# Moving the shift of a normalised piece from GpSimd to ScalarE, and giving GpSimd more pieces

## What is computed

```python
def first_block(x, ...):
    h = rmsnorm(x, norm_mix_g)             # MIX
    x = x + mixer(h) @ w_out
    h = rmsnorm(x, norm_ffn_g)             # FFN
    x = x + (silu(dwconv(h @ w_gate)) * (h @ w_up)) @ w_down
    return rmsnorm(x, norm_final_g)        # FIN1

def second_block(x, c, ...):
    # a layer that pools, then a layer of attention; shift and scale come from c
    h = rmsnorm(x, norm_g[0]) * (1 + scale) + shift      # POOL (together with FIN1)
    x = x + gate * pool_mixer(h, ...)
    hk = rmsnorm(x, kv_norm_g) * (1 + scale) + shift     # KV
    k, v = split(hk @ w_kv)
    h = rmsnorm(x, norm_g[1]) * (1 + scale) + shift      # ATT
    x = x + gate * swa_sink_mixer(h, k, v, ...)
    return rmsnorm(x, final_g)                           # FIN2
```

## Time and profile before

| | |
|---|---|
| median of 3 runs | 2089.77 us (2089.43 to 2089.9) |
| the profiled execution | 2088.51 us |
| its span in the trace | 2086.8 us |
| PE busy | 2064.3 us, 99% |
| DVE busy | 1231.7 us, 59% |
| ACT busy | 650.7 us, 31% |
| POOL busy | 748.9 us, 36% |

### The profile page before, as it was taken

The page is one execution under the profiler, slowest core; times in us unless marked ns, Lnnn a source line. Parts: engine busy times, 40 slices in busy tenths (PEclk is TensorE's granted clock), DMA queues, the critical chain, the costliest instruction groups (busy, mean ns, idle before and its releaser), DMA issues.

```text
span 2086.8 us, 24768 instructions
## 1 busy us (share of the span) xinstructions
PE 2064.3 (99%) x9344; PEld 1694.1 (81%) x9344; DVE 1231.7 (59%) x1698; ACT 650.7 (31%) x1089; POOL 748.9 (36%) x441
## 2 busy tenths in 40 slices
PE   8999999999999999999999999999999999999998
PEld 7888888888888888888878888888888878777886
DVE  7999776555644456445676453453463570697565
ACT  7323345221122211222254122122121261676112
POOL 4555626222221222212276122122131462565623
PEclk9999999999999999999999999999999999999999
DMA  4231112322133222332112121121121120010202
GB/s 154 72 111 41 41 51 91 121 101 97 63 111 111 101 85 76 109 112 101 41 41 61 38 64 41 41 60 40 40 61 41 41 71 31 21 42 21 71 11 81
DMA packets 44749, 141.26 MB, mean 68 GB/s; under 512 B 5616, under 2 KB 9856, under 8 KB 44672
## 3 DMA queue, kind: packets, MB, share of 16 engines
q1 hardware_dynamic: 31632, 100.68, 15.1%
q10 hardware_dynamic: 13040, 39.54, 5.2%
HBM read 135.98 MB, written 7.36 MB: 69 GB/s over the span
## 4 chain that ended last, share of the span: by engine, by line
PE 80%; DVE 12%; POOL 4%; ACT 2%; issue 1%; DMA 0%; POOLq 0%; SPq 0%; ACTq 0%; DVEq 0%
PE psum L594 24%; PE psum L596 24%; PE psum L595 24%; DVE psum L1651 7%; POOL temp L444 2%; PE psum L932 1%; PE psum L943 1%; DVE psum L1504 1%; DVE norm_lo L1517 1%; POOL w_lo L409 1%; PE psum L911 1%; PE psum L661 1%; POOL ada_raw L444 0%; PE psum L663 0%; PE psum L662 0%
## 5 line engine op out<-in xcount | busy, mean ns | idle before, releaser
L409 POOL TENSOR_TENSOR w_lo<-w_raw,w_hi 128x1024 fp32r<-128x1024 f32 x174 | 441.6, 2554 | 972.5 <-ACT w_hi L1036 967.0
L594 PE MATMUL psum<-norm_hi,w_hi 128*128 128x512 f32 x1632 | 636.3, 390 | 0.3 <-ACT temp L1104 0.3
L596 PE MATMUL psum<-norm_hi,w_lo 128*128 128x512 f32 x1632 | 635.0, 389 | 0.0
L595 PE MATMUL psum<-norm_lo,w_hi 128*128 128x512 f32 x1632 | 634.9, 389 | 0.0
L594 PEld LDWEIGHTS psum<-norm_hi,w_hi 128*128 128x128 f32 x1632 | 306.4, 188 | 64.7 <-issue 0.9
L596 PEld LDWEIGHTS psum<-norm_hi,w_lo 128*128 128x128 f32 x1632 | 306.4, 188 | 63.8
L595 PEld LDWEIGHTS psum<-norm_lo,w_hi 128*128 128x128 f32 x1632 | 306.4, 188 | 63.3 <-issue 0.2
L1104 ACT ACTIVATE temp<-psum 128x512 f32<-128x512 f32 x160 | 93.9, 598 | 420.6 <-PE psum L596 393.7
L1567 DVE SCALAR_TENSOR_TENSOR stream<-psum,mods,stream 128x512 f32<-128x512 f32 x160 | 119.7, 750 | 172.5 <-PE psum L596 172.5
L1036 ACT CAST w_hi<-w_raw 128x1024 fp32r<-128x1024 f32 x158 | 159.2, 1047 | 138.8 <-PE psum L596 79.6
L1565 DVE TENSOR_TENSOR stream<-psum,stream 128x512 f32<-128x512 f32 x176 | 118.7, 689 | 83.8 <-PE psum L596 83.6
(11 more groups left out here) (214 smaller groups left out, 2974.7 us busy)
## 6 DMA issues: line engine op xcount, KB each, us to landing
w_raw<-in_slabs SPq DMA_DIRECT2D x175, 512.0 KB, 3.5
ada_raw<-in_ada ACTq DMA_DIRECT2D x10, 3072.0 KB, 12.6
stream<-in_x SPq DMA_DIRECT2D x8, 512.0 KB, 9.3
out<-stream SPq DMA_DIRECT2D x8, 512.0 KB, 2.8
skew_scratch<-row_scratch ACTq DMA_DIRECT2D x1, 3072.0 KB, 17.6
ada_raw<-in_ada ACTq DMA_DIRECT2D x1, 2048.0 KB, 7.9
bias<-skew_scratch ACTq DMA_DIRECT2D x4, 512.0 KB, 4.2
c_act<-in_c ACTq DMA_DIRECT2D x1, 512.0 KB, 9.7
```

The lines of the kernel that those rows point to most:

```text
L409: nc.gpsimd.tensor_tensor(WL[place][:, :], RAW[at % 2][:, :], WH[place][:, :].bitcast(f32), ALU.subtract).then_inc(slab_ready, 1)
L594: nc.tensor.matmul(dst, wh, xh, start=n == 0, stop=False)
L595: nc.tensor.matmul(dst, wh, xl, start=False, stop=False)
L596: last = nc.tensor.matmul(dst, wl, xh, start=False, stop=n == len(terms) - 1)
```

## The change

Five edits:

- The shift of a piece of `POOL_LOWS` is no longer added by POOL. ACT does it, in place, in an instruction of its own right behind the cast of the same piece; that instruction waits for this cast. POOL is left with one instruction for each such piece.
- `POOL_LOWS` grows: for FFN from 3 pieces to 5, for the pooling norm from 3 to 5, for KV from 3 to 5, for ATT from 4 to 7. They are now the odd pieces, from 7 on (in ATT from 1 to 13). POOL's program is laid out anew for them, and the low part of a weight slab stands behind the new pieces in places.
- In FIN2 the squares of pieces 14 and 15 go to two buffers that were free, so ACT no longer waits for POOL's sums there.
- POOL sums pieces 8 to 11 only. DVE adds the squares of 13 and 14 to that of 12, between its last additions to the stream. PE sums three tensors as before: POOL's sum, DVE's, and the square of 15.
- The second half of the result goes out in 8 transfers of one piece instead of 4 of two, piece 14 ahead of piece 13.

```diff
@@ squares, POOL_LOWS @@
+            if n == FIN2 and m > 13:
+                return body(T[1], m % 2)
...
-        POOL_LOWS = [(MIX, m) for m in (2, 4, 6, 9, 11, 13)] + [(FFN, m) for m in (9, 11, 13)] + [(POOL, m) for m in (9, 12, 15)]
-        POOL_LOWS += [(KV, m) for m in (9, 12, 15)] + [(ATT, m) for m in (1, 4, 10, 13)]
+        POOL_LOWS = [(MIX, m) for m in (2, 4, 6, 9, 11, 13)] + [(FFN, m) for m in (7, 9, 11, 13, 15)]
+        POOL_LOWS += [(POOL, m) for m in (7, 9, 11, 13, 15)] + [(KV, m) for m in (7, 9, 11, 13, 15)]
+        POOL_LOWS += [(ATT, m) for m in (1, 3, 5, 7, 9, 11, 13)]
@@ sync @@
-            for half in range(2):
-                for k in range(0, KT, 2):
-
-                    sp.wait_ge(stream_normed, 16 + min(8 * half + k + 2, POOL_FROM))
...
+            for k in range(0, KT, 2):
+                sp.wait_ge(stream_normed, 16 + k + 2)
+                sp.dma_start(out[:, k:k + 2, hs(0)], X[:, k:k + 2, hs(0)]).then_inc(out_done, 16)
+            for k in (0, 1, 2, 3, 4, 6, 5, 7):
+                sp.wait_ge(stream_normed, 16 + 8 + min(k + 1, POOL_FROM - 8))
+                if k + 8 >= POOL_FROM:
+                    sp.wait_ge(pool_normed, k + 9 - POOL_FROM)
+                sp.dma_start(out[:, k:k + 1, hs(1)], X[:, k:k + 1, hs(1)]).then_inc(out_done, 16)
@@ gpsimd, piece_low @@
                 if shift(n, k) is not None:
-                    nc.gpsimd.tensor_tensor(src, src, shift(n, k).to_broadcast([P, HALF]), ALU.add).then_inc(pool_shifted, 1)
                     gp.wait_ge(pool_shifted, pool_lows(n, m) - pool_lows(FFN, 15))
@@ gpsimd @@
+            piece_low(POOL, 7)
             lows(POOL_SLAB + 2, POOL_SLAB + 3)
             piece_low(POOL, 9)
+            piece_low(POOL, 11)
             lows(POOL_SLAB + 3, POOL_SLAB + 4)
-            piece_low(POOL, 12)
+            piece_low(POOL, 13)
             piece_low(POOL, 15)
...
-            sums(FIN2, (az_done, 8), last=14)
+            sums(FIN2, (az_done, 8), last=12)
@@ tensor @@
-            pe.wait_ge(sum_done, 14 * SUMS_BEFORE[FIN2] + 12)
-            for n, summed in enumerate((sum_place(FIN2, 1), squares(FIN2, 14), squares(FIN2, 15))):
...
+            pe.wait_ge(sum_done, 14 * SUMS_BEFORE[FIN2] + 7 + 3)
+            for n, summed in enumerate((sum_place(FIN2, 1), squares(FIN2, 12), squares(FIN2, 15))):
+                if n == 1:
+                    pe.wait_ge(last_sum, 2)
@@ scalar, hi @@
                 else:
                     nc.scalar.activation(HH[:, k, hs(half)], piece(n, m), ACT.Identity, bias=shift(n, k)
                                          ).then_inc(hi_done, 1)
+                    if (n, m) in POOL_LOWS:
+                        act.wait_ge(hi_done, APPLIED_BEFORE[n] + m + 1)
+                        nc.scalar.activation(piece(n, m), piece(n, m), ACT.Identity, bias=shift(n, k)
+                                             ).then_inc(pool_shifted, 1)
@@ vector @@
+                if j > 29:
+                    m = j - 17
+                    dve.wait_ge(square_done, 16 * SUMS_BEFORE[FIN2] + m + 1)
+                    if j == 31:
+                        dve.wait_ge(last_sum, 1)
+                    nc.vector.tensor_tensor(squares(FIN2, 12), squares(FIN2, 12), squares(FIN2, m), ALU.add
+                                            ).then_inc(last_sum, 1)
```

More of the change, by code:

```diff
@@ L226, in build @@
             sem(n) for n in ("square_done", "sum_done", "stat_done", "root_done", "rstd_done"))
-        table_loaded = sem("table_loaded")
+        table_loaded, last_sum = sem("table_loaded"), sem("last_sum")
         squared_gain, rooted_gain = sem("squared_gain"), sem("rooted_gain")
@@ L382, in _ @@
                     sp.dma_start(RAW[n][:, :], slab_in[2 * i + n + 1, :, :]).then_inc(raw_ready[n], 16)
-            for half in range(2):
-                for k in range(0, KT, 2):
-                    sp.wait_ge(stream_normed, 16 + min(8 * half + k + 2, POOL_FROM))
[L387 to L390, removed]
+            for k in range(0, KT, 2):
[6 more added lines that the diff above has]
+                sp.dma_start(out[:, k:k + 1, hs(1)], X[:, k:k + 1, hs(1)]).then_inc(out_done, 16)
+            sp.wait_ge(out_done, 192)
         @block.gpsimd
@@ L513, in _ @@
             sums(FFN)
[L514 to L517, removed]
+            lows(FFN_SLAB + 2, FFN_SLAB + 3)
+            piece_low(FFN, 7)
+            lows(FFN_SLAB + 3, FFN_SLAB + 4)
+            for m in (9, 11, 13, 15):
+                piece_low(FFN, m)
             lows(FFN_SLAB + 4, FFN_SLAB + 6)
@@ L539, in _ @@
             sums(KV)
+            piece_low(KV, 7)
             lows(ATT_SLAB + 2, ATT_SLAB + 3)
             piece_low(KV, 9)
+            piece_low(KV, 11)
             lows(ATT_SLAB + 3, ATT_SLAB + 4)
-            piece_low(KV, 12)
-            piece_low(KV, 15)
-            piece_low(ATT, 1)
+            for n, m in ((KV, 13), (KV, 15), (ATT, 1), (ATT, 3)):
+                piece_low(n, m)
             lows(ATT_SLAB + 4, ATT_SLAB + 5)
-            piece_low(ATT, 4)
+            piece_low(ATT, 5)
+            piece_low(ATT, 7)
             lows(ATT_SLAB + 5, ATT_SLAB + 6)
-            piece_low(ATT, 10)
-            piece_low(ATT, 13)
+            for m in (9, 11, 13):
+                piece_low(ATT, m)
             lows(ATT_SLAB + 6, ATT_SLAB + 8)
@@ L1014, in _ @@
             pe.wait_ge(stream_normed, 16 + 8)
-            pe.wait_ge(sum_done, 14 * SUMS_BEFORE[FIN2] + 12)
-            for n, summed in enumerate((sum_place(FIN2, 1), squares(FIN2, 14), squares(FIN2, 15))):
-                if n:
-                    pe.wait_ge(square_done, 16 * SUMS_BEFORE[FIN2] + 14 + n)
+            pe.wait_ge(sum_done, 14 * SUMS_BEFORE[FIN2] + 7 + 3)
+            for n, summed in enumerate((sum_place(FIN2, 1), squares(FIN2, 12), squares(FIN2, 15))):
+                if n == 1:
+                    pe.wait_ge(last_sum, 2)
+                elif n == 2:
+                    pe.wait_ge(square_done, 16 * SUMS_BEFORE[FIN2] + 16)
                 for b in range(4):
@@ L1045, in square @@
                 at = 14 * SUMS_BEFORE[n] + 7 * half
-                if k >= 2:
+                if n == FIN2 and m > 13:
+                    pass
+                elif k >= 2:
                     act.wait_ge(sum_done, at + k - 2 + (1 if k == 2 else 0))
```

## The result

The changed kernel takes 2095.26 us, the median of 10 executions (2094.26 to 2095.89), against 2089.6 us for the kernel before on the same chip (2088.66 to 2092.22). The ratio is 1.0025, with a 95% interval of 1.0016 to 1.0035: slower by 0.25%. The predicted time was 2095.4. The profiled execution took 2095.66 us with a span of 2093.7; before it was 2088.51 with 2086.8.

The account below looks back on a forecast made before the run. PE, busy 99% of the span, was taken to bound the kernel. Stall +4.4, clock +1.4, pooling norm +1.2 and end -1.4 make +5.6: 2088.51 becomes 2094.1, plus 1.26 gives 2095.4 us, range 2091.8 to 2097.5.

Parts of the forecast that it names:

- ACT's cost of a shift: KV and ATT: each shift takes 0.75 us more on ACT, bounds 0.63 to 0.84; 11 stand ahead of the read.
- +4.4: ATT: PE starts its second half 4.4 us later, behind ACT's late read of the values product; bounds +3.1 to +5.4.
- The clock: ATT: behind PE's long wait seven matmuls start at half clock, +1.4 us; ends 0 and 2.8.
- the rival in which it stays up: ATT: the same stall of PE without a fall of the clock, +4.2, 2094.0 us; chance 0.22.
- The pooling norm: A weight slab's late low part delays a load, ACT's cast and the reads behind it: +1.2 us; ends 0 and 2.5.
- FFN: FFN: two more pieces on POOL cost nothing, or 1.3 us if PE's lead over the low parts were gone.
- The end: Behind the last product: earlier sums and single transfers begin and end the output 1.4 us earlier; ends -0.7 and -1.9.
- the rival with slower singles: The end: single transfers run below the pairs' rate, so it gives +0.4 instead of -1.4, 2097.2 us; chance 0.05.
- The sum: Whole kernel: +4.4 + 1.4 + 1.2 - 1.4 = +5.6 us on the profiled execution, 2088.51 to 2094.1.
- The added 1.26: Whole kernel: the runs' median lies 1.26 us above the profiled execution, so 2094.1 becomes 2095.4.
- the case that it is taken from: Cheaper shifts (+3.1), no clock loss, 0 for the slab, end -1.4: 2091.5 us; chance 0.08.

Follow-up runs that it names:

- t3: The change, but in ATT ACT makes all five reads of the second keys and values product ahead of the cast of piece 8: 2089.70 us, ratio 0.9999.
- t7: t5, but in ATT the five reads of the second keys and values product stand behind the casts of pieces 5 to 9: 2085.38 us, ratio 0.9978.
- t5: The change with POOL_LOWS and POOL's order of the kernel before; shifts on ACT and the new end stay: 2091.95 us, ratio 1.0010.
- t4: The change, but in the pooling norm POOL makes the low part of slab POOL_SLAB+3 ahead of that of piece 11: 2093.81 us, ratio 1.0020.
- t12: The change, but the five reads of the second keys and values product stand behind the casts of pieces 7 to 11: 2093.70 us, ratio 1.0020.
- t1: The kernel before with only the edits of the end (squares, sums and single outputs): 2088.69 us, ratio 0.9997.
- t8: t1, but in ATT the five reads of the second keys and values product stand behind the casts of pieces 5 to 9: 2087.32 us, ratio 0.9987.

## Why the prediction was right

- **ACT's cost of a shift.** Predicted 0.75 each, bounds 0.63 to 0.84. Where one can be read by itself it is 0.76 (the row at 1697.54); as a mean over the stretch it is 0.67 of busy time, 0.70 with the short gaps ahead of the shifts. 1.43 stay idle, 1.0 without these gaps, where I had 1.0. The read came 3.90 later by ACT's window, and PE's start 3.77 later counted from 1668: **+4.4 was +3.8**, inside +3.1 to +5.4; PE's idle stretch was 3.73, where I had 4.1. t3 shows that it is this read and its place.
- **The clock.** It fell, as the forecast had it; the rival in which it stays up does not hold for the change. The Trainium skill, page "TensorE: Matmul & The Clock Gate", section "HAM oscillation — how this bites in real kernels", says that a long wait puts the engine back to the half clock; the trace agrees for this wait, 3.73 us with a granted clock of 0.50 behind it. The term was mis-sized: 13 slow starts and not seven, **+2.6 and not +1.4**, near the upper end of the range given. The row that I took it from, the first 50 us, was a poor measure of the length: the profiles with a wait of 3.7 to 4.4 here show 8 to 14 slow starts. I also misread that place when I called PE less dense there: from 12 to 32 us it was busy in 4.00 of each 4.00 us.
- **The pooling norm.** **+1.2 was +2.0** in this profile and +1.6 as a mean over four; with the load in the chain taken off (4.09 here, 3.53 in before) it is +1.5, and +1.4 as a mean over the four. The chain ran as it was followed: the low part of the slab at 1074.75 (predicted 1074.6), the cast at 1078.59 (1078.3), DVE's first pooling step 1.22 later counted from 1047 (1.2; this step then took 1.44 instead of 1.23), the wait near 1113 at 1.18 (1.5). What I left out is that PE itself, at 1081.31, waits for the read of a tile that stands behind this cast; this adds nothing, since the start near 1113 hangs on the chain. I had said 3 us for the cast's wait; it was 2.11, since ACT, with the shifts in its queue, came to it 1.1 later.
- **FFN.** Nothing, as predicted: no wait for POOL's low parts appears in it, in this or any other kernel with the new table.
- **The end.** **-1.4 was -1.5.** The group of 16 starts at 1.83 behind the last product's start, as worked out, and the transfers are issued 1.36 earlier. Singles kept the rate of pairs, 380 GB/s, and the rival with slower singles falls. The rule of the Trainium skill, page "DMA: Bandwidth & Descriptors", section "Bandwidth", that transfers want 1 MiB, is not borne out by these rows, of transfers issued back to back on one queue. My price for that rival, three quarters of the pairs' rate, was no reading of the rule, which names a share of the peak.
- **The sum.** +5.6 was predicted for the profiled execution and +7.15 measured there (2088.51 to 2095.66): 1.6 too low, made of +0.8 in the pooling stage, -0.6 at the wait, +1.2 of clock, and small ones (0.2 ahead of 1047, 0.25 in what lies around the span, -0.25 behind 1870, -0.1 at the end). About 1.0 of it (0.56 of the load, the 0.2 and the 0.25) lies where executions of one kernel differ. The added 1.26 was the distance of the three runs' median from the profiled execution of before; the changed kernel's median lies 0.4 below its profiled one instead. So the two errors, 1.6 too low and 1.7 too high, cancel, and that the median of 2095.26 came within 0.2 of 2095.4 is luck. Between the medians of ten executions each (2089.6 and 2095.26) the difference is +5.7. What the terms had right is which stages lose and why; the wait was 0.6 too large and the clock's term 1.2 too small. The low end of the range, 2091.8, does not follow either: the case that it is taken from sums to 2091.5.

The step that would have served better is the one before the sum. I priced the new wait where the change put it, and didn't ask whether the read could stand elsewhere. t3 and t7 say that this was the question for whoever makes the change.

## What to carry to other kernels

On an engine that works in order, look for the one instruction that frees a buffer for the bottleneck, and count what stands ahead of it; that, and not the engine's busy share of 31%, prices the work that is added. Move such a read to the first place where its input is ready before you add work in front of it: here an earlier place was worth 1.1 us by itself and turned a loss of 0.1% (t5) into a gain of 0.22% (t7). A low part of a weight slab that is moved back by some instructions delays the load two slabs on, so follow it through the raw buffer to the casts and reads queued behind that load.

## What the runs showed of the hardware

- PE's clock behind a wait, in this one place and in one profile each: waits of 0.8 to 1.6 and of 2.88 left the granted clock at 1.00 in the windows behind them; waits of 3.72, 3.73, 3.75 and 4.45 were followed by windows at 0.50 to 0.60. For nearly the same wait (3.72 in t4, 3.73 in the change) the number of slow starts was 8 and 13, so the cost differed by 1 us. The length of the wait alone does not decide it: in the first 50 us of before a wait of 2.72 had 0.50 behind it, where the 2.88 of t12 had 1.00.
- Behind the last product the granted clock goes to 0.50 in every profile, but not at the same point. In t12 it is 0.73 from 2079.15 to 2080.15 and 0.50 behind that, while the 16 small matmuls run; in the change it is 1.00 until 2083.17, when most of them are done. The 16 took 1.95 to 1.97 in most profiles, but 2.61, 2.69 and 3.03 in t3, t4 and t12, and there the stretch to the end of the span was 14.2 to 14.55 instead of 13.0 to 13.5. The row of t12:

```profile
2078.98 3.03 PE L1030 MATMUL psum<-ones,temp 128*128 128x1 f32 x16 [0.66 <-DVE temp L2022]
```

- The product near 1113 waited 0.30 in before, 0.39 in t1 and 1.03 in t8, with the same instructions up to there. The slab load in the chain ahead of it took 3.53, 3.62 and 4.26. A single profile can't tell a change of this wait by less than about 0.7 us from nothing, unless the load is taken off: then five profiles with the same instructions agree within 0.1 us.
- Single transfers of 256 KB reached the rate of pairs of 512 KB, 380 and 376 GB/s.
